# The first tile's second half of a scaled addition on GpSimd, at the end of three stages, the rest on VectorE

## The chip, the cores and the metric

The kernel runs on one core of one Trainium2 chip. The time is the device time of one execution in microseconds; lower is better. A core has a matrix engine (TensorE, PE in the profile), VectorE (DVE), ScalarE (ACT), GpSimd (POOL) and SyncE (SP), which here only issues DMAs. The engines run their own instruction streams and wait for each other on semaphores.

## The reference, cut to what matters

Two transformer-like blocks over 256 tokens of 1024 features. What matters here is the second block, all in float32:

```python
h = rms_norm(x, ffn1_pre_g)
x = x + 0.5 * rms_norm(swiglu(h, ffn1_w_gate, ffn1_w_up, ffn1_w_down), ffn1_post_g)
h = rms_norm(x, mix_pre_g)
...                                    # attention and a state-space mixer on h
x = x + rms_norm(mixed, mix_post_g)    # mixed = concat(attn, ssm) @ w_out
h = rms_norm(x, ffn2_pre_g)
x = x + 0.5 * rms_norm(swiglu(h, ffn2_w_gate, ffn2_w_up, ffn2_w_down), ffn2_post_g)
```

So three times a product y of a stage is normed and added to the rows: x = x + c * rs * (y * g), where g is a gain for each feature and rs the reciprocal root for each token.

## The kernel before, in words

The rows X lie in SBUF as two tiles of 128 tokens, X[:, tt, :], each 1024 wide; tt is the tile, hf the half of 512 features. The weights stream in by DMA from SyncE, ScalarE rounds each part to a high part (whi) and VectorE makes the rest (wlo); TensorE multiplies with both. The order on each engine is written out by hand, and semaphores link them.

At the end of a stage four products, one for each (tt, hf), stand in four PSUM banks (fa0 to fa3, wm0 to wm3, fb0 to fb3). `post_norm(i, names, loads)` (line 1827) on VectorE adds them to X. i is 4 behind the first feed-forward, 6 behind the mixing stage and 8 behind the second feed-forward. Its steps:

- `tile_mean` (1810, instruction 1814) prepares the first sum of squares of a tile; ScalarE makes the sums in `tile_stats` (1380) and the root in `tile_root` (1371).
- `gained(n)` (1836) multiplies bank n by the gain PG into the buffer XN2, 128x512.
- `tile_scale` (1820) takes the reciprocal of the root: the scale of each token, nst[:, i % 2, 8 + tt].
- `piece(n)` (1844) is one instruction on 128x512: X = XN2 * scale + X. It counts up the semaphore x_piece.

In VectorE's order: mean 0, gained 0, gained 1, scale 0, piece 0, piece 1, mean 1, gained 2, scale 1, piece 2, gained 3, piece 3. Behind stages 4 and 6 VectorE then waits for all pieces and counts up x_half and x_new, which release ScalarE's sums of squares for the next norm (1354).

Behind stages 4 and 6 TensorE turns X by `tile_transposes` (line 726; its instructions are 739, fillers 704): tile 0 half 0, tile 0 half 1, then tile 1 half 0 and half 1, each group of four transposes waiting for its piece by x_piece. Three filler matmuls stand before each group of tile 1. ScalarE copies the turned banks into XT's high part (`stream_hi`, 1412), and VectorE makes the low part (`stream_lo`, 1897), pair by pair; a pair can start only when tile 1's group has been turned too. Behind stage 4 VectorE first makes the small weights of the next product (`small_parts`, 1906 and 1907), TensorE waits for them, runs five fillers (704, ten records) and goes on.

Behind stage 8 X goes out in four stores of 256 KB: SyncE's two (line 627, half 0 of both tiles) wait for x_piece 9 and 11, ScalarE's two (line 1763, half 1) for x_piece 10 and 12.

GpSimd's last work in the kernel before is a set of masks near 877 us (lines 679 to 694); it is idle after that.

Of the kernel before, what the change touches and what calls it, by code (L numbers as in the profile page):

```python
# [8 lines left out]
T, D = 256, 1024  # L9
# [17 lines left out]
PIECES = {(0, 0): 2, (1, 0): 3, (1, 2): 3}  # L27
# [181 lines left out]
def before_in(ring, n):  # L209

    return next((m for m in range(n - 1, -1, -1) if ring[m] == ring[n]), None)
# [44 lines left out]
def reads_upto(i, who):  # L256

    return sum(1 for _, e in MAIN[:i + 1] if e == who)


def program(nc, x, panels1, experts, peer_u, peer_v, ffa, panels2, ffb, cols, conv_cols, w_low, w_gate_up, w_sgu, k12,
# [3 lines left out]
    ALU = mybir.AluOpType  # L265
# [5 lines left out]
    with ctx:  # L271
        def sb(name, shape, dt=f32):
            return ctx.enter_context(nc.sbuf_tensor(name, shape, dt))

        def sem(name):
            return ctx.enter_context(nc.semaphore(name))
# [9 lines left out]
        X = sb("X", [P, NT, D])  # L286
# [12 lines left out]
        nst = small[:, 0:20].rearrange("p (a n) -> p a n", a=2)  # L299
# [83 lines left out]
        XN2 = cut(NT, D)  # L383
# [55 lines left out]
        t_done = sem("t_done")  # L439
        t_read = [sem("t_read_0"), sem("t_read_1")]  # L440
        norm_sq, norm_ms, norm_sd, norm_out = sem("norm_sq"), sem("norm_ms"), sem("norm_sd"), sem("norm_out")
        x_new, x_half, x_piece = sem("x_new"), sem("x_half"), sem("x_piece")
        yf_ready, rs_ready, rs_spread = sem("yf_ready"), sem("rs_ready"), sem("rs_spread")
        gla_abs, gla_ln, gla_l, gla_e = sem("gla_abs"), sem("gla_ln"), sem("gla_l"), sem("gla_e")
        gla_kd, gla_state = sem("gla_kd"), sem("gla_state")
# [35 lines left out]
        def read_out(eng, name):  # L481

            i = MAIN_AT[name]
            who = MAIN[i][1]
            eng.wait_ge(main_read[who], reads_upto(i, who))
# [9 lines left out]
        def t_claim(pe, stage, j):  # L495

            i = before_in(T_BANK, T_AT[stage] + j)
            if i is not None:
                t_read_wait(pe, i)
# [75 lines left out]
        @block.sync  # L575
        def _(sp):
            for tt in range(NT):
                sp.dma_start(X[:, tt, :], x[0, P * tt:P * tt + P, :]).then_inc(x_in[tt], 16)
            sp.dma_start(C[:, 0:NCOLS], cols[:, 0:NCOLS]).then_inc(cols_in, 16)
            sp.dma_start(FINAL, cols[:, NCOLS:NCOLS + 8]).then_inc(cols_in, 16)  # L580
            sp.dma_start(WL, w_low).then_inc(low_in, 16)

            def wait_item_used(item):

                n = item - EXP0
                if n < 0:
                    sp.wait_ge(part_lo, 2 * item + 2)
                elif n < P // 2:
                    sp.wait_ge(h_done, 2 * n + 2)
                elif n < P:  # L590
                    sp.wait_ge(a_used, 2 * n + 2 - P)
                else:
                    sp.wait_ge(part_lo, 2 * (item - P) + 2)

            def load(item, src):
                before = before_in(ITEM_SLOT, item)
                if before is not None:
                    wait_item_used(before)
                sp.dma_start(raw[:, ITEM_SLOT[item], :], src).then_inc(slot_ready[ITEM_SLOT[item]], 16)

            for j in range(EXP0):
                load(j, panels1[j])

            def stream(item0, count, src, split0):

                for j in range(RING):
                    load(item0 + j, src[j])
                turns = (count - RING) // RING
                with sp.Fori(0, turns, 1) as i:
                    for s in range(RING):  # L610

                        sp.wait_ge(part_lo, i * (2 * RING) + (split0 + 2 * s + 2))
                        slot = ITEM_SLOT[item0 + s]
                        sp.dma_start(raw[:, slot, :], src[i * RING + (RING + s)]).then_inc(slot_ready[slot], 16)
                for j in range(RING * (turns + 1), count):
                    load(item0 + j, src[j])

            for j in range(P):
                load(EXP0 + j, experts[j])
            sp.dma_start(FG, row_post[0:1, :].broadcast_to([P, D])).then_inc(final_in, 16)  # L620
            stream(FFA0, FFI, ffa, S_FFA)
            for j in range(FFB0 - MIX0):
                load(MIX0 + j, panels2[j])
            stream(FFB0, FFI, ffb, S_FFB)
            for tt in range(NT):
                sp.wait_ge(x_piece, 8 + 2 * tt + 1)
                sp.dma_start(out[0, P * tt:P * tt + P, 0:512], X[:, tt, 0:512]).then_inc(out_done, 16)
            sp.wait_ge(out_done, 16 * 2 * NT)

# [2 lines left out]
        def _(pool):  # L632
# [36 lines left out]
            for n in range(2 * PICKS):  # L669
                if n >= BUFS:  # L670
# [23 lines left out]
            pool.affine_select(out=DB[:, P:384], in_=DB[:, P:384], compare_op=ALU.is_ge, fill=-1e32, base=P,  # L694
                               pattern=[[-1, T]], channel_multiplier=1).then_inc(pool_const2, 1)

        @block.tensor
        def _(pe):  # L700
            def keep_busy(out, n):

                for _ in range(n):
                    pe.matmul(out[:, 0:P], ident[:, :], ident[:, :], start=True, stop=True)
# [21 lines left out]
            def tile_transposes(stage, src, arrive, scales=None, order=range(NT), keep={}):  # L726

                pairs = dict(TSTAGES)[stage]
                for j in range(pairs):
                    t_claim(pe, stage, j)  # L730
                for tt in order:
                    for j in range(pairs):
                        keep_busy(t_bank(stage, pairs - 1 if (tt, j) == (1, 2) else 0)[:, P:2 * P], keep.get((tt, j), 0))
                        arrive(tt, j // 2)
                        for q in range(2):
                            c = slice(P * (2 * q + tt), P * (2 * q + tt) + P)
                            k = 2 * j + q
                            if scales is None:
                                last = pe.transpose(t_bank(stage, j)[:, c], src[:, tt, P * k:P * k + P], ident[:, :])
                            else:  # L740
                                last = pe.matmul(t_bank(stage, j)[:, c], src[:, tt, P * k:P * k + P], scales[:, tt, :],
                                                 start=True, stop=True)
                        if tt == order[-1]:
                            last.then_inc(t_done, 1)

            def tiles(src, n):

# [416 lines left out]
            feed_forward(S_FFA, 0, [f"fa{i}" for i in range(4)], between=lambda: (turn_back(2), turn_back(3)))  # L1164


            tile_transposes("mix", X, lambda tt, hf: pe.wait_ge(x_piece, 2 * tt + hf + 1), keep=PIECES)
            new_stream("mix")
            pe.wait_ge(small_split, 2)
            claim(pe, "dt")  # L1170
# [109 lines left out]
            for j in range(1, 4):  # L1280
# [10 lines left out]
            pe.wait_ge(part_lo, S_WM + 12)  # L1291
            last_two([bank(name) for name in names], (S_WM + 10, S_WM + 11), (stream_acts(NK - 2), stream_acts(NK - 1)),
                     part_used)
            tile_transposes("ffb", X, lambda tt, hf: pe.wait_ge(x_piece, 4 + 2 * tt + hf + 1), keep=PIECES)
            new_stream("ffb")
            feed_forward(S_FFB, NF, [f"fb{i}" for i in range(4)])

# [2 lines left out]
        def _(act):  # L1300
# [458 lines left out]
            warm_root(1)  # L1759
            tile_stats(8, *products_of("fb"))  # L1760
            for hf in range(2):
                act.wait_ge(x_piece, 8 + 2 * hf + 2)
                act.dma_start(out[0, P * hf:P * hf + P, 512:D], X[:, hf, 512:D]).then_inc(out_done, 16)


# [1 line left out]
        def _(dve):  # L1767
# [49 lines left out]
            def tile_scale(i, tt):  # L1817

                dve.wait_ge(norm_sd, NORM_ROOTS[i] + tt + 1)
                link(dve.reciprocal(nst[:, i % 2, 8 + tt:9 + tt], nst[:, i % 2, 6 + tt:7 + tt]))  # L1820
# [6 lines left out]
            def post_norm(i, names, loads):  # L1827

                dve.wait_ge(post_in, 16 * loads)

                def gained(n):

                    tt, hf = n // 2, n % 2
                    dve.wait_ge(main_done, MAIN_AT[names[n]] + 1)
                    dve.wait_ge(norm_sq, sum(NORM_PARTS[:i]) + n + 1)
                    read_done(dve.tensor_tensor(XN2[:, tt, 512 * hf:512 * hf + 512], bank(names[n]),
                                                PG[:, 512 * hf:512 * hf + 512], ALU.mult))

                def piece(n):

                    tt, hf = n // 2, n % 2
                    c = slice(512 * hf, 512 * hf + 512)
                    read_out(dve, names[n])
                    dve.scalar_tensor_tensor(X[:, tt, c], XN2[:, tt, c], nst[:, i % 2, 8 + tt:9 + tt], X[:, tt, c],
                                             ALU.mult, ALU.add).then_inc(x_piece, 1)

                tile_mean(i, 0, 1)
                gained(0)
                gained(1)
                tile_scale(i, 0)  # L1850
                piece(0)
                piece(1)
                tile_mean(i, 1, 3)
                gained(2)
                tile_scale(i, 1)
                piece(2)
                gained(3)
                piece(3)
                if i != 8:
                    dve.wait_ge(x_piece, 4 if i == 4 else 8)  # L1860
                    dve.sem_inc(x_half, 1)
                    dve.sem_inc(x_new, 1)

# [168 lines left out]
            for i in range(4):  # L2032
                hf, tt = i // 2, i % 2
# [656 lines left out]
```

## Time and profile before

| | us |
|---|---|
| median of 3 runs | 1432.86 (1432.69 to 1433.44) |
| the profiled execution | 1431.76 |
| its span, first to last instruction | 1430.0 |
| TensorE busy | 1398.2 (98%) |
| VectorE busy | 1021.1 (71%) |
| ScalarE busy | 521.8 (36%) |
| GpSimd busy | 274.9 (19%) |

All times of the trace are from the start of the span. A row of a timeline gives the start, the duration, the engine, the line, the operation, output and inputs by name with their shapes, how many instructions were merged, and in brackets the idle time ahead of it and who ended it. Two instructions of an engine can overlap in the records by about 0.1 us, since the next one starts while the last one drains. PE is the matmul record and PEld the weight load of the same instruction. The mean granted clock of TensorE was 0.999 of full speed, and everything ran on the one core.

### The profile page before, as it was taken

How to read it: one execution, taken by the hardware profiler on the slowest of the kernel's cores; microseconds unless marked ns; L12 is line 12 of the kernel's file. 1: busy time of each engine (PE TensorE's matmuls, PEld its weight loads, DVE VectorE, ACT ScalarE, POOL GpSimd, SP SyncE). 2: the span in 40 equal slices, each digit the busy share in tenths (PEclk: the TensorE clock that was granted, in tenths of full speed). 3: DMA queues.
4: the chain of work that ended last, by engine and by line, in shares of the span. 5: the costliest groups of instructions: out<-in, count | busy, mean ns of one | idle time of the engine just before them, and what ended most of it. 6: DMA issues, size and time to landing. Idle time of an engine off the chain costs nothing.

```text
span 1430.0 us, 23127 instructions
## 1 busy us (share of the span) xinstructions
PE 1398.2 (98%) x9058; PEld 1285.1 (90%) x9058; DVE 1021.1 (71%) x1836; ACT 521.8 (36%) x953; POOL 274.9 (19%) x235
## 2 busy tenths in 40 slices
PE   8999999999999999999999999999999999999998
PEld 7788889999999999999999998888889978888886
DVE  5566747989888886544444527788789897687887
ACT  5545464311433332000000006444457586544444
POOL 1000036344255454433333300000000000000000
PEclk9999999999999999999999999999999999999999
DMA  6445444699999999999999985555444333455552
GB/s 235 177 147 179 175 154 156 220 415 408 367 369 377 371 364 394 416 415 414 417 414 415 414 345 181 205 199 181 176 165 168 125 106 111 167 203 194 187 194 89
DMA packets 67211, 372.13 MB, mean 260 GB/s; under 512 B 7969, under 2 KB 8481, under 8 KB 34866
## 3 DMA queue, kind: packets, MB, share of 16 engines
q1 hardware_dynamic: 37440, 266.45, 49.0%
q0 software_dynamic: 27648, 100.68, 18.0%
q10 hardware_dynamic: 2034, 3.76, 0.7%
q8 instruction: 62, 1.02, 0.3%
q14 instruction: 27, 0.22, 0.0%
HBM read 369.81 MB, written 1.05 MB: 259 GB/s over the span
## 4 chain that ended last, share of the span: by engine, by line
PE 67%; DVE 14%; DMA 10%; ACT 6%; issue 3%; POOL 0%; DVEq 0%; SPq 0%; ACTq 0%; POOLq 0%
PE ps L754 26%; PE ps L1064 11%; PE ps L787 11%; PE ps L1013 10%; DMA raw<-in_experts 9%; PE ps L789 5%; ACT xt_plain L1527 3%; DVE wlo L569 2%; DVE hi_plain L2087 2%; DVE xt_plain L2201 2%; DVE lo_plain L2087 2%; DVE arena L2190 1%; DVE XT L1897 1%; PE ps L786 1%; DVE arena L2512 1%
## 5 line engine op out<-in xcount | busy, mean ns | idle before, releaser
L1064 PE MATMUL ps<-arena,raw 128*128 128x160 f32 x2048 | 282.1, 300 | 6.5 <-DMA raw<-in_experts 6.4
L1064 PEld LDWEIGHTS ps<-arena,raw 128*128 128x128 f32 x2048 | 278.6, 190 | 9.9 <-issue 6.0
L1013 PE MATMUL ps<-arena,raw 128*128 128x160 f32 x2048 | 284.8, 300 | 2.1 <-DVEq L2182 0.9
L1013 PEld LDWEIGHTS ps<-arena,raw 128*128 128x128 f32 x2048 | 279.2, 190 | 4.8 <-issue 2.1
L787 PE MATMUL ps<-XT,whi 128*128 128x512 f32 x704 | 249.5, 399 | 1.2 <-DVE wlo L569 1.0
L552 ACT ACTIVATE whi<-raw 128x1024 fp32r<-128x1024 f32 x152 | 159.7, 1060 | 237.5 <-PE ps L754 108.8
L569 DVE TENSOR_TENSOR wlo<-raw,whi 128x1024 fp32r<-128x1024 f32 x138 | 167.2, 1221 | 81.1 <-ACT whi L552 80.2
L754 PE MATMUL ps<-whi,XT 128*128 128x512 f32 x592 | 184.8, 393 | 3.3 <-DVE XT L1897 1.5
L789 PE MATMUL ps<-XT,wlo 128*128 128x256 f32 x616 | 172.8, 281 | 0.0
L1621 ACT ACTIVATE whi<-raw 128x1024 fp32r<-128x1024 f32 x96 | 101.9, 1062 | 155.7 <-PE ps L787 101.6
L787 PEld LDWEIGHTS ps<-XT,whi 128*128 128x128 f32 x704 | 129.4, 188 | 28.3 <-DVE wlo L569 2.1
L2364 DVE TENSOR_TENSOR wlo<-raw,whi 128x1024 fp32r<-128x1024 f32 x96 | 117.3, 1222 | 44.4 <-ACT whi L1621 44.4
L754 PEld LDWEIGHTS ps<-whi,XT 128*128 128x128 f32 x592 | 109.4, 188 | 30.6 <-issue 4.7
L754 PE MATMUL ps<-XT,whi 128*128 128x256 f32 x640 | 117.2, 285 | 2.7 <-DVE wlo L569 1.0
L789 PEld LDWEIGHTS ps<-XT,wlo 128*128 128x128 f32 x616 | 116.4, 189 | 3.2
L754 PE MATMUL ps<-wlo,XT 128*128 128x512 f32 x296 | 115.4, 390 | 0.0
L2108 DVE SCALAR_TENSOR_TENSOR arena<-hi_plain,arena 128x1024 f32<-128x1024 f32 x46 | 59.1, 1284 | 78.7 <-DMA hi_plain<-in_peer_v,arena 78.6
L2108 DVE SCALAR_TENSOR_TENSOR arena<-lo_plain,arena 128x1024 f32<-128x1024 f32 x47 | 60.4, 1285 | 63.7 <-DMA lo_plain<-in_peer_v,arena 63.0
L754 PEld LDWEIGHTS ps<-XT,whi 128*128 128x128 f32 x640 | 99.5, 192 | 3.7 <-issue 1.9
L754 PE MATMUL ps<-XT,wlo 128*128 128x256 f32 x320 | 90.5, 283 | 0.0
L672 POOL DMA_INDIRECT hi_plain<-in_peer_u,arena x48 | 69.0, 1438 | 105.8 <-DVE arena L2087 77.4
L672 POOL DMA_INDIRECT lo_plain<-in_peer_u,arena x48 | 62.1, 1293 | 59.4 <-DVE arena L2087 48.8
(312 smaller groups left out, 1861.4 us busy)
## 6 DMA issues: line engine op xcount, KB each, us to landing
raw<-in_experts SPq DMA_DIRECT2D x128, 1024.0 KB, 8.0
raw<-in_panels SPq DMA_DIRECT2D x58, 1024.0 KB, 4.9
raw<-in_ffa SPq DMA_DIRECT2D x33, 1024.0 KB, 4.9
raw<-in_ffb SPq DMA_DIRECT2D x33, 1024.0 KB, 4.8
arena<-in_row_post ACTq DMA_DIRECT2D x4, 512.0 KB, 4.9
X<-in_x SPq DMA_DIRECT2D x2, 512.0 KB, 5.3
hi_plain<-in_peer_u,arena POOLq DMA_INDIRECT x48, 9.0
lo_plain<-in_peer_u,arena POOLq DMA_INDIRECT x48, 9.9
```

The costliest lines, as they stand in the source:

```text
L552: act.activation(whi[:, buf(p), :], half(item_of(p), p % 2), ACT.Copy).then_inc(part_hi, 1)
L569: eng.tensor_tensor(low_weights(p), half(item_of(p), p % 2), whi[:, buf(p), :].bitcast(f32), ALU.subtract).then_inc(part_lo, 1)
L672: pool.indirect_dma_start(out=GATHERED[n % BUFS], out_offset=None, in_=(peer_u, peer_v)[n // PICKS][:, :], in_offset=bass.IndirectOffsetOn ...
L754: last = pe.matmul(out, x if w_moving else w, w if w_moving else x, start=start and n == 0, stop=stop and n == 2)
L787: last = pe.matmul(out, wh[:, k], XT[:, k], start=k == 0, stop=k == NK - 1)
L789: pe.matmul(out[:, T:], wl[:, k], XTh[:, k], start=False, stop=False)
L1013: last = pe.matmul(out[:, 0:TD], w[:, k], XF[:, k, :], start=k == 0, stop=k == NK - 1)
L1064: last = pe.matmul(t_bank("ffa", k // 2)[:, at:at + TD], w[:, P * k:P * k + P], G[:, c, :], start=False, stop=False, skip_group_check=True)
L1621: act.activation(whi[:, buf(q), :], half(item_of(q), q % 2), ACT.Copy)\
L2087: dve.tensor_tensor_reduce(u, u, XROWS[:, k // 32, :], 1.0, 0.0, ALU.mult, ALU.add, HS[:, k:k + 1])\
L2108: ins = dve.scalar_tensor_tensor(into, v, a, into, ALU.mult, ALU.add)
L2364: dve.tensor_tensor(wlo[:, buf(q), :], half(item_of(q), q % 2), whi[:, buf(q), :].bitcast(f32), ALU.subtract).then_inc(part_lo, 1)
```

## The change

In `post_norm` piece 1 (tile 0, half 1) leaves VectorE. GpSimd does it in two instructions, a scale of XN2 in place and an addition to X, with a wait on its own semaphore between them. It waits until VectorE has read all of bank 1 (`read_out`) and for the new semaphore first_scaled, which VectorE counts up behind scale 0 and ahead of piece 0; it counts up x_second. The counts of x_piece go from four to three for each stage, and whoever waited for the moved piece waits for x_second: TensorE's second group of tile 0, ScalarE's first store, and VectorE ahead of x_half and x_new. At stage 8 SyncE's two stores wait for counts 7 and 8 instead of 9 and 11.

```diff
             for tt in range(NT):
-                sp.wait_ge(x_piece, 8 + 2 * tt + 1)
+                sp.wait_ge(x_piece, 6 + tt + 1)
                 sp.dma_start(out[0, P * tt:P * tt + P, 0:512], X[:, tt, 0:512]).then_inc(out_done, 16)
...
+            for stage, i in enumerate((4, 6, 8)):
+                read_out(pool, ("fa1", "wm1", "fb1")[stage])
+                pool.wait_ge(first_scaled, stage + 1)
+                pool.tensor_scalar(XN2[:, 0, 512:D], XN2[:, 0, 512:D], nst[:, i % 2, 8:9], None, ALU.mult)\
+                    .then_inc(x_scaled, 1)
+                pool.wait_ge(x_scaled, stage + 1)
+                pool.tensor_tensor(X[:, 0, 512:D], X[:, 0, 512:D], XN2[:, 0, 512:D], ALU.add).then_inc(x_second, 1)
...
+            def piece_in(stage, tt, hf):
+
+                if (tt, hf) == (0, 1):
+                    pe.wait_ge(x_second, stage + 1)
+                else:
+                    pe.wait_ge(x_piece, 3 * stage + (1, 2, 3)[tt + hf])
...
-            tile_transposes("mix", X, lambda tt, hf: pe.wait_ge(x_piece, 2 * tt + hf + 1), keep=PIECES)
+            tile_transposes("mix", X, lambda tt, hf: piece_in(0, tt, hf), keep=PIECES)
...
-            tile_transposes("ffb", X, lambda tt, hf: pe.wait_ge(x_piece, 4 + 2 * tt + hf + 1), keep=PIECES)
+            tile_transposes("ffb", X, lambda tt, hf: piece_in(1, tt, hf), keep=PIECES)
...
             for hf in range(2):
-                act.wait_ge(x_piece, 8 + 2 * hf + 2)
+                act.wait_ge(*((x_piece, 9) if hf else (x_second, 3)))
                 act.dma_start(out[0, P * hf:P * hf + P, 512:D], X[:, hf, 512:D]).then_inc(out_done, 16)
...
                 tile_scale(i, 0)
+                dve.sem_inc(first_scaled, 1)
                 piece(0)
-                piece(1)
                 tile_mean(i, 1, 3)
...
                 if i != 8:
-                    dve.wait_ge(x_piece, 4 if i == 4 else 8)
+                    dve.wait_ge(x_piece, 3 if i == 4 else 6)
+                    dve.wait_ge(x_second, 1 if i == 4 else 2)
                     dve.sem_inc(x_half, 1)
                     dve.sem_inc(x_new, 1)
```

## Rows read from the trace of the kernel before

**Rows 1.** The page's busy times: us, share of the span, instructions.
```profile
PE 1398.2 (98%) x9058; PEld 1285.1 (90%) x9058; DVE 1021.1 (71%) x1836; ACT 521.8 (36%) x953; POOL 274.9 (19%) x235
```

**Rows 2.** Busy time by stretch: us, then each engine, TensorE's clock, DMA.
```profile
1056.00:1062.00 6.00, 5.38 (x38) 4.22 (x37) 5.59 (x13) 4.79 (x13) 0.00 (x0) 1.00 0.06 25
1233.00:1238.00 5.00, 4.64 (x35) 3.88 (x35) 4.59 (x11) 3.57 (x10) 0.00 (x0) 1.00 0.00 2
```

**Rows 3.** The chain that ended last, behind stage 4: start, us, what.
```profile
1060.82 0.02 DVEq L1862
...
1060.94 0.30 DVE HAh L1906
...
1061.27 0.43 DVE HAl L1907
...
1061.74 1.38 PE ps L704 x10
```

**Rows 4.** Timeline of VectorE behind stage 4.
```profile
1056.16 0.15 DVE L1820 RECIPROCAL small<-small 128x1 f32<-128x1 f32 x1
1056.35 1.42 DVE L1844 SCALAR_TENSOR_TENSOR X<-arena,small,X 128x512 f32<-128x512 f32 x2
1057.68 0.15 DVE L1814 TENSOR_SCALAR small<-small 128x1 f32<-128x1 f32 x1
...
1058.34 0.15 DVE L1820 RECIPROCAL small<-small 128x1 f32<-128x1 f32 x1
1058.53 0.75 DVE L1844 SCALAR_TENSOR_TENSOR X<-arena,small,X 128x512 f32<-128x512 f32 x1
...
1059.92 0.75 DVE L1844 SCALAR_TENSOR_TENSOR X<-arena,small,X 128x512 f32<-128x512 f32 x1
```

**Rows 5.** Timeline of TensorE's weight loads behind stage 4.
```profile
1057.82 0.42 PEld L739 LDWEIGHTS ps<-ident,X 128*128 128x128 f32 x4 [0.25 <-DVE X L1844]
1058.21 0.75 PEld L704 LDWEIGHTS ps<-ident 128*128 128x128 f32 x6
1059.34 0.42 PEld L739 LDWEIGHTS ps<-ident,X 128*128 128x128 f32 x4 [0.38 <-DVE X L1844]
...
1060.72 0.42 PEld L739 LDWEIGHTS ps<-ident,X 128*128 128x128 f32 x4 [0.25 <-DVE X L1844]
```

**Rows 6.** Timeline of ScalarE behind stage 4.
```profile
1057.24 0.19 ACT L1380 ACTIVATION_READ_ACCUMULATOR arena<-ps 128x1 f32 x1
1057.87 0.29 ACT L1371 ACTIVATE small<-small 128x1 f32<-128x1 f32 x1 [0.43 <-DVE small L1814]
```

**Rows 7.** GpSimd's groups: busy us, mean ns of one, idle before.
```profile
L694 POOL TENSOR_SCALAR_AFFINE_SELECT arena<-arena 128x256 f32<-128x256 f32 x1 | 0.4, 400 | 0.0
...
L692 POOL TENSOR_SCALAR_AFFINE_SELECT arena<-arena 128x128 f32<-128x128 f32 x1 | 0.3, 293 | 0.0
```

**Rows 8.** Lines by source (ns min/median/max), and both engines' timelines near 200 us.
```profile
L569 POOL TENSOR_TENSOR wlo<-raw,whi x14: 2377/2393/3377, 200.6 to 241.1; 128x1024 fp32r<-128x1024 f32 x14
...
200.64 5.72 POOL L569 TENSOR_TENSOR wlo<-raw,whi 128x1024 fp32r<-128x1024 f32 x2 [180.00 <-ACT whi L552]
...
200.88 3.22 DVE L2070 SCALAR_TENSOR_TENSOR arena<-X,small,arena 96x1024 f32<-96x1024 f32 x1 [2.49 <-DMA arena<-in_row_post]
...
L2108 DVE SCALAR_TENSOR_TENSOR arena<-hi_plain,arena x46: 1283/1284/1287, 575.0 to 835.2; 128x1024 f32<-128x1024 f32 x46
```

**Rows 9.** Timeline behind stage 6: ScalarE's root, its copies, VectorE's low parts.
```profile
1233.81 0.29 ACT L1371 ACTIVATE small<-small 128x1 f32<-128x1 f32 x1 [0.72 <-DVE small L1814]
...
1235.76 3.03 ACT L1412 ACTIVATE XT<-ps,C 128x256 fp32r<-128x256 f32 x8 [0.71 <-PE ps L739]
...
1236.96 3.22 DVE L1897 SCALAR_TENSOR_TENSOR XT<-ps,C,XT 128x256 fp32r<-128x256 f32 x8 [0.34 <-DVE X L1844]
```

**Rows 10.** The last addition, and landing time of ScalarE's stores (line 1763).
```profile
1426.79 0.75 DVE L1844 SCALAR_TENSOR_TENSOR X<-arena,small,X 128x512 f32<-128x512 f32 x1
...
DMA to landing us min/median/max: 2.0/2.0/2.0
```

More of the change, by code:

```diff
@@ L441, in program @@
         norm_sq, norm_ms, norm_sd, norm_out = sem("norm_sq"), sem("norm_ms"), sem("norm_sd"), sem("norm_out")
-        x_new, x_half, x_piece = sem("x_new"), sem("x_half"), sem("x_piece")
+        x_new, x_half, x_piece, x_second = sem("x_new"), sem("x_half"), sem("x_piece"), sem("x_second")
+        first_scaled, x_scaled = sem("first_scaled"), sem("x_scaled")
         yf_ready, rs_ready, rs_spread = sem("yf_ready"), sem("rs_ready"), sem("rs_spread")
```

## The prediction

> **What bounds the kernel now.** Start at the busy shares: TensorE is busy for 98% of the span and GpSimd for 19% [rows 1]. So time can be won or lost only where TensorE waits. The change touches three such places, the ends of stages, where the normed product is added to the rows X: after the first feed-forward (A, 1054 to 1062 us), after the mixing stage (B, 1230 to 1240 us) and after the second feed-forward (C, 1421 to the end). The stretches by time show TensorE 5.4 of 6 us busy in A and 4.6 of 5 us in B, at a granted clock of 1.00, with GpSimd idle [rows 2]; part of TensorE's work there is filler. The chain of waits says who leads in A: VectorE, link after link, up to the low part of the small weights at 1061.27; TensorE's fillers start 0.04 us after that ends [rows 3]. The VectorE timeline shows what it does in A: scale of tile 0, two additions of 0.75 us back to back (1.42 together, so the next may start 0.67 after the first), the mean and product of tile 1, its scale, two more additions [rows 4]. The TensorE loads show its side: four transposes take 0.39, three fillers 0.75, and the waits for X are only 0.25 and 0.38 [rows 5]. So two transpose groups of tile 1 can't start closer than 1.14 us apart.
>
> **What the change removes, adds and moves, in A.** *Removed:* the second addition of tile 0, 0.67 us of VectorE. Not all of it comes back. Scale 1 needs ScalarE's root, which waited 0.43 us for VectorE's mean; its fourth sum was there at 1057.43 [rows 6]. With 0.10 for its own wait (estimate: 0.04 from the mean's end to the root in rows 4 and 6, taken higher) the root starts at 1057.53 instead of 1057.87. Gain on VectorE: 0.34, and piece 2 becomes due at 1058.19 instead of 1058.53.
>
> *Added on VectorE:* one semaphore step ahead of piece 0. The step at 1060.82 held the next instruction to 1060.94 [rows 3]: 0.12. Behind it stand piece 0 and all that follows, but as the root is set by ScalarE, the 0.12 only moves piece 0 to 1056.47 and is hidden by the root's wait (without that cover, 0.12 each time). At stages A and B the extra wait on GpSimd ahead of the two steps that release the norm of the next stage costs nothing as long as GpSimd ends before piece 3.
>
> *Added on GpSimd:* a scale and an addition of 128x512, one after the other. No such scale stands in the trace. Its nearest rows are the one-input selects: 400 ns for 256 elements and 293 for 128 [rows 7], 0.84 ns an element, so 0.61 for 512; with the scale read from memory I take 0.7 (bounds 0.6 and 1.2, the addition's). The addition: 2393 ns for 1024 elements [rows 8], so between 1.2 (half) and 1.34 (with 0.29 of it fixed, which is about what the 128-element select takes in all); I take 1.3. Between the two 0.1 for the semaphore.
>
> *Do they run beside VectorE?* This decides the case, and one place in the trace answers it. At 200.88 VectorE starts a three-operand addition of 96x1024, two inputs in SBUF, while GpSimd is in a subtraction since 200.64. It takes 3.22 us; the same form elsewhere takes 1284 ns [rows 8]. So its work ran from 202.82, 0.2 before GpSimd's 2.38 us (the group's least) was over at 203.02; and GpSimd's next subtraction took 3377 instead of 2393. One blocked the other, both ways. Pieces 0, 2 and 3 are of that form; the products with a PSUM input, the means and the reciprocals are not, and I take them as free.
>
> The Trainium skill, SBUF — State Buffer, "Who interferes with whom", says it as a rule against this change: a VectorE instruction with two SBUF inputs and a GpSimd instruction that reads SBUF exclude each other, and whichever starts first keeps the port to its end. The trace agrees, with 3.22 against 1.28 us. By that rule the sum is the forecast below; were it not so, the rival "no block" would be.
>
> **The sum.** In A, VectorE first: piece 0 holds GpSimd's scale back to 1057.2; scale to 1057.9; addition 1058.0 to 1059.3, and VectorE may go on at 1059.1. Piece 2, due at 1058.19, waits 0.9 and ends at 1059.85 instead of 1059.28. Gained 0.34, lost 0.91: pieces 2, 3 and the small weights come 0.57 later. TensorE: tile 0's second group starts at 1059.35, tile 1's groups 1.14 and 2.28 later, at 1060.49 and 1061.63 instead of 1059.34 and 1060.72. The last is 0.91 late, but TensorE stood idle after it until 1061.74 [rows 3, 5], so the stage is late by the small weights: **+0.57**.
>
> B is the same with times 175.95 later. There the root waited longer, 0.72 [rows 9], so its new start is set by the mean and piece 2 is due at 1233.95, just when GpSimd's addition starts (1233.95): close to a tie. If GpSimd's comes first, tile 1's first group starts at 1236.44 instead of 1235.28 (1.16 late), ScalarE's first two copies of the stream, 1235.76 before, end near 1237.67, and VectorE's first low part, 1236.96 before [rows 9], starts near 1237.70: **+0.75**. No slack follows, since from there the chain runs on VectorE into TensorE.
>
> C: the end is piece 3 at 1426.79 and the store behind it, 2.0 us [rows 10]. The store of tile 0's second half moves to about 1426.2, still ahead of piece 3 (1427.4) on ScalarE's queue, and nothing is queued behind it but the last store. SyncE's two stores count one piece less and move with piece 2. So the end moves with piece 3: **+0.57**.
>
> Sum 0.57 + 0.75 + 0.57 = 1.9 us. The profiled execution took 1431.76 (span 1430.0 and 1.76 around it), so it would be 1433.7; the median of the three runs was 1432.86, 1.1 more, so I forecast 1434.8. What a measurement of this kernel can tell from no change is about 0.2%, 2.87 us: up to 1435.73 counts as the same.
>
> **The rivals.**
> - *GpSimd first (0.24).* Its scale and piece 0 are released within a few hundredths of each other, and no row says who wins. If the scale does, it runs 1056.45 to 1057.15, piece 0 ends at 1057.7, GpSimd's addition runs 1057.65 to 1058.95, the mean comes at 1057.62, nearly as before, piece 2 is due at 1058.47, waits to 1058.75 and pieces 2 and 3 end 0.2 to 0.3 late. In B tile 1's first group is 0.9 late and the stream 0.45. Together 0.3 + 0.45 + 0.3 = +1.1: 1434.0.
> - *Slower by over 0.2%: piece 2 slips in between scale and addition (0.20).* This happens where GpSimd's scale takes over about 0.9 us in A (over 0.7 in B), or starts late. Then the addition starts only after piece 2, at 1058.94, and ends at 1060.3. VectorE loses little (piece 3 waits to 1060.1), but TensorE's three groups start at 1060.35, 1061.49 and 1062.63; the fillers follow at 1063.03 instead of 1061.74, +1.3. In B the same +1.5 through the stream (first group 1237.24, low part 1238.5). In C +0.2 to 0.4, since the last two stores then go out nearly together. Sum +3.1: 1436.0. For it: the scale's price is an extrapolation. Against it: the one-input rows are short. Where it happens in B alone the sum is 0.57 + 1.5 + 0.57 = 2.6, 1435.5.
> - *No block (0.10).* If GpSimd's addition takes in only what it needs and VectorE isn't held, pieces 2 and 3 come 0.34 early: A -0.3, C -0.3. GpSimd ends at 1058.6 (0.7 + 0.1 + 1.3 after 1056.5), tile 1's groups come 0.45 and 0.3 late, which is within TensorE's idle time in A and about nothing in B. Sum -0.6: 1432.3. Against it: the 3.22 us in rows 8.
> - *A granted clock that falls (0.03).* TensorE will wait 1.6 us in one piece for tile 0's second half. Rows 2 show 1.00 through the present, shorter gaps. If half the clock doubled the 2.28 us of transposes and fillers behind it (an estimate; no row shows such a stretch), half of that beyond TensorE's slack, about 1 us would be added in each of A and B: 1436.8.
>
> **How the numbers follow.** Forecast 0.43 (the sum of B's two forms lies in 1434.8 to 1435.5), GpSimd first 0.24, piece 2 in between 0.20, no block 0.10, clock 0.03. The range of 8 in 10 leaves out most of the no-block case and the far end of the slow ones: 1432.6 to 1436.4. Slower by over 0.2%: most of the case in between (0.14), the clock (0.03) and a little of the forecast's upper form (0.04), 0.21. Faster by over 0.2% would need 2.87 us, while all that can be gained is 0.34 to 0.56 at each of three places: 0.03 for what I don't see. Same: 0.76.
>
> **What would show it.** In the profile after: GpSimd's scale (0.7, or 1.3 with the wait in it) and addition (1.3) three times; piece 0 at 750 ns (forecast) or near 1250 (GpSimd first); piece 2 near 1650 ns instead of 750, and 750 with a long piece 3 in the slow case; root 1 starting 0.34 earlier; TensorE waiting 1.6 us for GpSimd's addition at the second transpose group of tile 0; the last store 0.57 later after the last matmul. Pieces at 750 throughout would make the prediction wrong on its main point; a scale over 0.9 us would make it too low.

## The result, and the profile after

The median went from 1432.78 to 1440.2 us (four executions each): the ratio is 1.0048, with a 95% interval of 1.0036 to 1.006. The change makes the kernel slower by 7.4 us; 1.9 were forecast. The profiled execution took 1440.13, its span 1438.4.

The page's busy times, and GpSimd's two new groups (busy us, mean ns of one, idle before), answer [rows 1] and [rows 7]:

```profile
PE 1398.9 (97%) x9058; PEld 1286.9 (89%) x9058; DVE 1020.5 (71%) x1833; ACT 522.1 (36%) x953; POOL 280.6 (20%) x241
...
L701 POOL TENSOR_SCALAR arena<-arena,small 128x512 f32<-128x512 f32 x3 | 6.3, 2112 | 542.0 <-DVEq L1866 542.0
L704 POOL TENSOR_TENSOR X<-X,arena 128x512 f32<-128x512 f32 x3 | 3.8, 1266 | 0.3
```

VectorE has three instructions less, as meant. But the scale takes 2.11 us on GpSimd, and no busy time has grown enough for 8.4 us of span.

**Where the time went.** Executions of this kernel differ by some us ahead of stage 4 already, in parts that the change leaves alone, so spans can't be compared here to a few tenths. What can be compared is the time from one stage's end to the next. As a mark I take ScalarE's first sum of squares in each of the three places. The timeline of ScalarE, before and then after:

```profile
1054.03 0.60 ACT L1380 ACTIVATE arena<-ps 128x512 f32<-128x512 f32 x1
...
1420.93 0.60 ACT L1380 ACTIVATE arena<-ps 128x512 f32<-128x512 f32 x1 [2.80 <-PE ps L754]
```

```profile
1055.01 0.60 ACT L1395 ACTIVATE arena<-ps 128x512 f32<-128x512 f32 x1
...
1231.61 0.60 ACT L1395 ACTIVATE arena<-ps 128x512 f32<-128x512 f32 x1 [1.63 <-PE ps L769]
...
1425.26 0.60 ACT L1395 ACTIVATE arena<-ps 128x512 f32<-128x512 f32 x1 [2.80 <-PE ps L769]
```

(The mark of B before is at 1229.68.) The differences, for every kernel of this study:

| kernel, profiled execution | A to B | B to C | C to the end |
|---|---|---|---|
| before | 175.65 | 191.25 | 9.07 |
| the change | 176.60 | 193.65 | 13.14 |
| e1, stages 4 and 6 only | 176.62 | 193.75 | 9.05 |
| e2, stage 8 only | 175.69 | 191.19 | 13.18 |
| e3, a memset at the end | 175.60 | 191.18 | 13.98 |
| e4, the change with fillers | 176.55 | 192.46 | 13.09 |
| e5, GpSimd instructions tried beside | 175.66 | 191.22 | 9.08 |
| e6, a memset at stage 6 | 175.62 | 191.21 | 9.03 |
| e7, scale released by piece 0 | 178.52 | 192.84 | 13.44 |
| e8, before without VectorE's steps | 175.30 | 190.60 | 9.06 |
| e9, GpSimd's addition alone, 4 and 6 | 175.65 | 191.45 | 9.07 |
| e10, e1 with fillers | 176.64 | 192.46 | 9.09 |
| e11, e3 without the gathers | 175.67 | 191.22 | 9.06 |
| e12, e9 without VectorE's steps | 174.91 | 191.29 | 9.03 |

Where nothing was changed the columns repeat within 0.09 us, over executions whose first mark lies anywhere from 1043.0 (e11) to 1061.0 (e5). e5, e6, e7, e9, e11 and e12 ran once each, with the profiler: 1438.72, 1433.28, 1441.32, 1432.74, 1420.64 and 1433.17 us. What they say is read from the columns; e5's 7 us and e11's 11 us lie ahead of A. The change costs 0.95 us behind stage 4 (A), 2.40 behind stage 6 (B) and 4.07 at the end (C), 7.4 together, which is the difference of the medians.

**In A**, the timelines of GpSimd, VectorE and TensorE's loads, answering [rows 4] and [rows 5]:

```profile
1057.54 2.11 POOL L701 TENSOR_SCALAR arena<-arena,small 128x512 f32<-128x512 f32 x1 [178.68 <-DVEq L1866]
1059.73 1.26 POOL L704 TENSOR_TENSOR X<-X,arena 128x512 f32<-128x512 f32 x1
...
1057.45 0.75 DVE L1859 SCALAR_TENSOR_TENSOR X<-arena,small,X 128x512 f32<-128x512 f32 x1 [0.16 <-DVE small L1835]
...
1059.03 0.75 DVE L1859 SCALAR_TENSOR_TENSOR X<-arena,small,X 128x512 f32<-128x512 f32 x1
...
1060.42 1.12 DVE L1859 SCALAR_TENSOR_TENSOR X<-arena,small,X 128x512 f32<-128x512 f32 x1
1062.20 0.30 DVE L1922 CAST HAh<-arena 128x256 fp32r<-128x256 f32 x1 [0.65 <-DVE X L1859]
...
1058.26 0.42 PEld L747 LDWEIGHTS ps<-ident,X 128*128 128x128 f32 x4 [0.32 <-DVE X L1859]
1061.05 0.42 PEld L747 LDWEIGHTS ps<-ident,X 128*128 128x128 f32 x4 [2.37 <-POOL X L704]
...
1063.21 0.47 PEld L747 LDWEIGHTS ps<-ident,X 128*128 128x128 f32 x4
```

VectorE's piece 0 starts 0.09 us ahead of GpSimd's scale. Piece 2 (1059.03) runs in 0.75 us beside the scale; piece 3 meets GpSimd's addition and takes 1.12. TensorE waits 2.37 us for the addition, and the groups of tile 1 follow it with no wait: the last of all groups starts 8.20 us behind the mark, 6.69 before.

VectorE's own chain did get shorter. The first product and ScalarE's root of tile 1 before, then the same and VectorE's second scale after:

```profile
1057.75 0.68 DVE L1836 TENSOR_TENSOR arena<-ps,arena 128x512 f32<-128x512 f32 x1
```

```profile
1058.19 0.68 DVE L1851 TENSOR_TENSOR arena<-ps,arena 128x512 f32<-128x512 f32 x1
1058.84 0.16 DVE L1835 RECIPROCAL small<-small 128x1 f32<-128x1 f32 x1
...
1058.51 0.29 ACT L1386 ACTIVATE small<-small 128x1 f32<-128x1 f32 x1
```

Before, the root was there at 1058.16 and the scale of tile 1 started at 1058.34, when VectorE came out of the product: the product held it, not the root. After, the root ends at 1058.80 and the scale follows 0.04 later. Behind the mark the root comes 0.34 earlier (3.50 against 3.84), and piece 2 comes 0.48 earlier (4.02 against 4.50).

**In B** the same gap of 2.36 us stands ahead of the second group, and the groups behind it are slow. TensorE's loads, and busy time by stretch (the last three columns are the granted clock, DMA share, GB/s), answering [rows 2]:

```profile
1237.61 0.64 PEld L747 LDWEIGHTS ps<-ident,X 128*128 128x128 f32 x4 [2.36 <-POOL X L704]
...
1239.52 0.87 PEld L747 LDWEIGHTS ps<-ident,X 128*128 128x128 f32 x4
```

```profile
1234.00:1236.00 2.00, 1.40 (x10) 0.93 (x8) 1.94 (x5) 1.91 (x6) 1.90 (x1) 1.00 0.02 4
1236.00:1238.00 2.00, 0.38 (x2) 0.39 (x3) 1.96 (x3) 0.35 (x1) 1.48 (x2) 0.94 0.02 4
1238.00:1240.00 2.00, 2.00 (x12) 2.00 (x11) 0.11 (x1) 0.00 (x0) 0.00 (x0) 0.50 0.00 0
1240.00:1242.00 2.00, 2.00 (x15) 2.00 (x14) 0.65 (x2) 1.60 (x5) 0.00 (x0) 0.71 0.00 0
```

Behind the gap the granted clock is 0.50, which is the level of 1.2 GHz, and four transposes take 0.87 us where the like group took 0.47 in A at 1.00 (1063.21).

VectorE's start in B also differs from before for a reason that the change doesn't contain. In the kernel before, 0.23 us pass between the first two products of B in which VectorE waits for nothing that the profile shows:

```profile
1231.50 0.69 DVE L1836 TENSOR_TENSOR arena<-ps,arena 128x512 f32<-128x512 f32 x1 [0.23 <-issue]
```

This idle time stands there in every execution in which VectorE's instructions up to B are those of before (before, e2, e3, e5, e6, e11), and in none of the others. Without it the scale of tile 0 comes 0.32 earlier behind the mark (2.11 in the change, 2.43 before). Why it goes is open; in B each kernel of the second kind has these 0.3 us of VectorE's chain to the good.

**At the end** the last piece is over at 1431.76, 6.50 us behind the mark, 0.11 earlier than before; ScalarE's stores land 2.1 us after they are issued. All that would end the program near 1434. It ends at 1438.4. The instructions that end the program stand under line 271, the `with ctx:` around the whole of it. GpSimd's drain, at the end of its stream, is one of them. Duration in ns, start in us, after:

```profile
L271 POOLq DRAIN  x1: 8258/8258/8258, 1429.9 to 1429.9; - x1
...
L271 SPq DRAIN  x1: 7/7/7, 1434.1 to 1434.1; - x1
...
L271 SPq EVENT_SEMAPHORE  x1: 17/17/17, 1438.3 to 1438.3; - x1
```

SyncE is done at 1434.1 and passes the common end at 1438.3. In between only GpSimd's drain is under way: it ends at 1438.16, 6.95 us behind GpSimd's last addition (1429.94 and 1.27). The same drain stands in the trace of the kernel before, behind the last mask (877.43 and 0.40), where nothing waited for it:

```profile
L271 POOLq DRAIN  x1: 7922/7922/7922, 876.9 to 876.9; - x1
```

### The profile page after: what moved, and what is told of

It reads as the page before. It is cut to its first block, busy times and chain, and to the rows that moved or that the text cites. A ratio compares the mean times of both kernels' runs of the same rounds, so it can differ in the third digit from the quotient of the medians.

```text
span 1438.4 us, 23133 instructions
## 1 busy us (share of the span) xinstructions
PE 1398.9 (97%) x9058; PEld 1286.9 (89%) x9058; DVE 1020.5 (71%) x1833; ACT 522.1 (36%) x953; POOL 280.6 (20%) x241
## 3 DMA queue, kind: packets, MB, share of 16 engines
HBM read 369.81 MB, written 1.05 MB: 258 GB/s over the span
## 4 chain that ended last, share of the span: by engine, by line
PE 65%; DVE 14%; DMA 11%; ACT 6%; issue 2%; POOL 1%; DVEq 0%; SPq 0%; ACTq 0%; POOLq 0%
PE ps L769 26%; DMA raw<-in_experts 11%; PE ps L802 11%; PE ps L1079 10%; PE ps L1028 10%; PE ps L804 5%; ACT xt_plain L1542 3%; DVE wlo L570 2%; DVE hi_plain L2103 2%; DVE xt_plain L2217 2%; DVE lo_plain L2103 2%; DVE arena L2206 1%; DVE XT L1913 1%; PE ps L801 1%; DVE arena L2528 1%
## 5 line engine op out<-in xcount | busy, mean ns | idle before, releaser
L701 POOL TENSOR_SCALAR arena<-arena,small 128x512 f32<-128x512 f32 x3 | 6.3, 2112 | 542.0 <-DVEq L1866 542.0
```

## The experiments

### The end: e1, e2, e3, e6, e11

e1 takes the change at stage 4 and 6 alone, e2 at stage 8 alone. The edit of e1 (e2 is its mirror; the counts of x_piece follow):

```diff
-            for stage, i in enumerate((4, 6, 8)):
+            for stage, i in enumerate((4, 6)):
...
-                dve.sem_inc(first_scaled, 1)
+                if i in (4, 6):
+                    dve.sem_inc(first_scaled, 1)
                 piece(0)
+                if i not in (4, 6):
+                    piece(1)
```

> The change at stages 4 and 6 alone; behind stage 8 VectorE does all four pieces again. Theory (the end's loss is GpSimd's drain, which lasts 6.95 us behind its last instruction and was hidden 540 us before the end): the last addition ends where it did and the span ends 2.4 us behind it, as before the change. Of the 7.4 us, 4.1 are gone: 1436.0, +3.3 against before (0.93 at stage 4, 2.4 at stage 6), less where TensorE's clock does not fall behind stage 6. Rival (the loss at the end is no drain but two stores that collide on ScalarE's queue): the same time here, so this run says only how much belongs to the end; the late memset tells the two apart. Rival (the whole is one loss before stage 8, by what GpSimd does to the weight stream): near 1440.

Measured: 1435.83 us, ratio 1.002 (1.001 to 1.003). The end is 9.05 as before, A and B are those of the change.

> The change at stage 8 alone. Theory (drain): GpSimd's addition ends some 0.1 us before the last piece and the program ends 6.95 us behind it instead of 2.4: +4.0 us, 1436.8, with the granted clock at 1.00 up to the last matmul. The two parts, this and the change at stages 4 and 6 alone, add up to the whole change (7.4). Rival (stores collide): the stores land over 4 us later than the last piece and the drain is short.

Measured: 1435.98 us, ratio 1.0025 (1.0014 to 1.0035), with 13.18 to the end and nothing in A and B. The columns add up: 0.97 + 2.50 + 4.11 is 7.6, for 7.4 of the whole. The medians, each against its own runs of before (1432.66), add up to 6.5 only (3.2 and 3.3), which their intervals allow. GpSimd's drain in e2 is as long as in the change, 8.26 us from the addition's start.

e3 tells drain from stores. One instruction is added to the kernel before, at the end of GpSimd's stream:

```diff
+            pool.wait_ge(x_piece, 12)
+            pool.memset(LS[:, 6:7], 0.0)
```

> The kernel before with one added instruction: a GpSimd memset of one unused column behind the last of the twelve additions. No work moves, nobody waits for it. Theory (GpSimd's drain at the program's end lasts 6.95 us from its last instruction): the memset ends near 1427.7 of the span, so the span ends near 1427.7 + 6.95 + 0.2 = 1434.9 instead of 1430.0: +4.9, 1437.7. Rival (the drain's length comes from the two big instructions, or the end is late because of the stores): the memset is over in 0.1 us and costs nothing, 1432.8.

Measured: 1437.67 us, ratio 1.0033 (1.0024 to 1.0043): +5.0, as the theory says, for a memset of 0.10 us that nobody waits for. Its drain, from line 271's instructions:

```profile
L271 POOLq DRAIN  x1: 7050/7050/7050, 1430.7 to 1430.7; - x1
```

e6 is the same memset behind the eighth addition (wait for x_piece 8), in the middle of the program.

> The kernel before with one added GpSimd memset of one unused column behind the eighth addition, at the end of stage 6, some 190 us before the end. Theory (a drain of 7 us behind GpSimd's last instruction, dear only where nothing else is left to do): the drain stands at 1237 to 1244 of the span and the last stage ends in 9.07 us from its first sum, as before. Rival (any late use of GpSimd lengthens the end by 4 to 5 us): 13 to 14.

Measured: 9.03 us from the mark of C to the end. The drain is as long, but stands under 190 us of other work:

```profile
L271 POOLq DRAIN  x1: 7050/7050/7050, 1238.2 to 1238.2; - x1
```

So the length of the drain is the same, and the place of GpSimd's last instruction decides what it costs. e11 asks what makes it long. It is e3 with the gathers gone:

```diff
-                pool.indirect_dma_start(
-                    out=GATHERED[n % BUFS], out_offset=None, in_=(peer_u, peer_v)[n // PICKS][:, :],
-                    in_offset=bass.IndirectOffsetOnAxis(ap=ROWS[:, n % PICKS:n % PICKS + 1], axis=0))\
-                    .then_inc(row_here[n % BUFS], 16)
+                pool.memset(GATHERED[n % BUFS], 0.5).then_inc(row_here[n % BUFS], 16)
```

> The run with the late memset again, with GpSimd's 192 gathers replaced by memsets of the same buffers, so the expert rows and the output are wrong. Theory (the drain is long because GpSimd has issued indirect DMAs; at the head of the program, ahead of any, it took 0.19 us): the drain behind the late memset takes well under 1 us and the last stage ends in 9.1 us from its first sum instead of 13.98. Rival (7 us is what a drain of GpSimd costs late in any program): 7.05 us and 13.98 as before. The stretch of the gathers itself gets shorter; that says nothing here.

Measured: the drain takes 0.17 us, and the end comes 9.1 us behind the mark (1409.84, span 1418.9).

```profile
L271 POOLq DRAIN  x1: 171/171/171, 1416.5 to 1416.5; - x1
```

The 7 us need the gathers, though the last of them is issued at 828 us (line 672 in the kernel before), 600 us earlier. Whether any DMA issued by GpSimd does it or only the indirect kind was not tried.

### The clock: e4 and e10

```diff
-PIECES = {(0, 0): 2, (1, 0): 3, (1, 2): 3}
+PIECES = {(0, 0): 2, (0, 2): 9, (1, 0): 3, (1, 2): 3}
```

> The whole change with nine more filler matmuls (some 2.3 us) on TensorE ahead of the second pair group of tile 0, behind stages 4 and 6, where TensorE idled 2.37 us for GpSimd. Theory (the wait itself costs 0.9 us behind stage 4 and about 1.1 behind stage 6, and the fall of the granted clock to 0.50 for 3.4 us behind stage 6 costs the other 1.3): the clock stays at 1.00, stage 6 costs about 1.1 instead of 2.4, and the time is 1438.8, 1.3 below the change; runs scatter less. Rival (the clock's fall is not what TensorE's chain waits for, or comes whatever fills the gap): 1440.1 as with the change.

Measured: 1439.21 us, ratio 1.0037 (1.0024 to 1.0049). The stretches behind stage 6, where the change had 0.50 and 0.71:

```profile
1240.00:1242.00 2.00, 1.88 (x18) 1.69 (x17) 0.85 (x1) 0.06 (x1) 0.30 (x1) 1.00 0.00 0
1242.00:1244.00 2.00, 1.99 (x19) 1.82 (x18) 1.11 (x3) 2.00 (x6) 0.00 (x0) 1.00 0.00 0
```

B to C is 192.46: B costs 1.21 and not 2.40. The clock's share there is 1.2 us. The medians (1440.2 and 1439.21) go the same way, but their intervals overlap; the column decides. e10 has the same fillers with the change at stages 4 and 6 alone.

> The change at stages 4 and 6 alone, with nine fillers on TensorE in the gap behind each. No drain at the end, no fall of the clock. Theory: from first sum to first sum 176.6 and 192.45, 9.05 to the end, +2.15 against before: 1434.8, and 1.2 us or a part of it below the same without fillers (1435.8). Rival (the fall of the clock doesn't come from the gap): a stretch at 0.50 still shows behind stage 4 or 6, and the time is that of the run without fillers.

Measured: 1435.77 us, ratio 1.0016 (1.0006 to 1.0026); the columns are those expected, 176.64, 192.46 and 9.09. The time is 1.0 above the forecast, with its own runs of before at 1433.31, 0.65 above those of e1. That the fillers are worth 1.2 in the median can't be told from these runs (e1 had 1435.83 without them). The gap does not always bring the fall: in the change and e1 it came in B and not in A, in e7 in A (A to B 178.52) and not in B, each with a gap of 2.4 to 2.7 us; with fillers in neither, in e4 and e10. e7's stretches in A, busy time and granted clock:

```profile
1061.00:1063.00 2.00, 1.84 (x10) 1.84 (x11) 1.31 (x3) 0.00 (x0) 0.10 (x1) 0.59 0.02 4
1063.00:1065.00 2.00, 2.00 (x12) 2.00 (x12) 0.25 (x2) 1.14 (x4) 0.00 (x0) 0.56 0.00 0
```

### GpSimd's prices: e5 and e7

e5 adds 29 instructions on free memory while GpSimd is idle anyway, four rounds of seven forms:

```diff
+            one(pool.memset(XS[:, 0, :], 1.0))
+            for _ in range(4):
+                one(pool.tensor_scalar(A, A, eps, None, ALU.mult))
+                one(pool.tensor_scalar(A, A, 1.5, None, ALU.mult))
+                one(pool.tensor_scalar(A[:, 0:256], A[:, 0:256], eps, None, ALU.mult))
+                one(pool.tensor_scalar(A[:, 0:256], A[:, 0:256], 1.5, None, ALU.mult))
+                one(pool.tensor_tensor(A, A, B2, ALU.add))
+                one(pool.tensor_tensor(A, A, eps.broadcast_to([P, 512]), ALU.mult))
+                one(pool.tensor_tensor(A[:, 0:256], A[:, 0:256], B2[:, 0:256], ALU.add))
```

> The kernel before with 29 added GpSimd instructions on free memory during the first feed-forward, one after the other: four times a scale of 128x512 with the factor read from memory, the same with a constant factor, both on 128x256, an addition of 128x512, a product of 128x512 with one column broadcast, an addition of 128x256. Theory (the scale is dear by its form, the factor from memory, and 2.11 us behind the stages is its own price): 2.1 us here too, about half with the constant, and the price hangs on the 512 elements (256 take about 1.2). Rival (its own price is about 0.7 and the rest was waiting for VectorE's additions, first piece 0 and then piece 2): the shortest of four is about 0.7 with either factor. The addition should take 1.27 where VectorE leaves it alone.

By source line, ns of the shortest, middle and longest of four: the scale with its factor from memory, with a constant, the latter on 256, and the addition:

```profile
L710 POOL TENSOR_SCALAR arena<-arena,C x4: 1616/1898/2853, 886.0 to 921.3; 128x512 f32<-128x512 f32 x4
L711 POOL TENSOR_SCALAR arena<-arena x4: 1491/1714/2127, 888.1 to 923.0; 128x512 f32<-128x512 f32 x4
...
L713 POOL TENSOR_SCALAR arena<-arena x4: 854/933/1914, 892.8 to 926.8; 128x256 f32<-128x256 f32 x4
L714 POOL TENSOR_TENSOR arena<-arena x4: 1278/1558/1697, 893.9 to 927.7; 128x512 f32<-128x512 f32 x4
```

Neither theory held as put. The scale's own price is 1.5 to 1.6 us, with either factor: not 2.1, and not 0.7. An element costs it 2.5 ns ((1491 - 854) / 256), three times the 0.84 of the selects in [rows 7]. The addition has the price forecast.

e7 says what the other 0.55 of the 2.11 is:

```diff
-                pool.wait_ge(first_scaled, stage + 1)
+                pool.wait_ge(x_piece, 3 * stage + 1)
```

> The whole change, but GpSimd's scale is released by piece 0's end instead of by the semaphore step ahead of it, so that it starts about 0.65 us later and never beside piece 0. Theory (the scale takes 2.11 by its form): it still takes 2.11, all behind it comes 0.65 later, and the stages cost 1.6 and 3.0 instead of 0.95 and 2.4. Rival (0.6 of the 2.11 was the wait for piece 0): it takes 1.5, ends where it did, and the stages cost 0.95 and 2.4 as with the change.

```profile
L701 POOL TENSOR_SCALAR arena<-arena,small x3: 1562/1564/1576, 1058.2 to 1429.5; 128x512 f32<-128x512 f32 x3
```

The rival held for the scale: 1.56 us. So 0.55 was the wait for piece 0, all three times. The stages' costs came as neither side put them. The release by piece 0 comes a little late, GpSimd's addition ends 0.3 later than in the change, and B, where the clock stayed at 1.00 here, costs 1.59: 0.3 more than e4's 1.21, and a little. A, where the clock fell, costs 2.87: without the change's 0.95 and the 0.3 of the later release, the fall is worth about 1.6 there (an estimate from these three).

### What a faster GpSimd would have given: e9 and e12

e9 is e1 without GpSimd's scale (three lines less), e12 takes VectorE's wait and steps behind piece 3 away as well, as e8 does.

> GpSimd at stages 4 and 6 only, and its scale left out: it adds the unscaled half to the rows, so the second half of tile 0 is wrong. GpSimd's part is then one addition, 0.1 + 1.26 us, with 0.55 of waiting for piece 0 ahead of it. Theory (the stages are late only because GpSimd's two instructions end 2.9 us later than VectorE's piece did, and VectorE's own chain did get shorter): the addition ends 3.9 us behind the stage's first sum instead of 5.98, TensorE's groups are 0.2 us late or less, the pieces 2 and 3 come 0.25 to 0.3 early, and stage 4 takes 175.4 from first sum to first sum against 175.65 before, stage 6 191.2 against 191.25. Rival (having GpSimd read beside VectorE costs VectorE more than the piece saved): stage 4 takes 176 or more.

The timelines of GpSimd and VectorE in A, then in B:

```profile
1057.33 1.84 POOL L701 TENSOR_TENSOR X<-X,arena 128x512 f32<-128x512 f32 x1 [178.74 <-DVEq L1865]
...
1057.28 0.75 DVE L1857 SCALAR_TENSOR_TENSOR X<-arena,small,X 128x512 f32<-128x512 f32 x1 [0.16 <-DVE small L1833]
...
1232.94 1.27 POOL L701 TENSOR_TENSOR X<-X,arena 128x512 f32<-128x512 f32 x1 [173.77 <-DVEq L1865]
...
1232.89 1.86 DVE L1857 SCALAR_TENSOR_TENSOR X<-arena,small,X 128x512 f32<-128x512 f32 x1 [0.16 <-DVE small L1833]
```

The two exclude each other, and here both orders are seen: in A VectorE goes through in 0.75 and GpSimd takes 1.84 instead of 1.27; in B GpSimd goes through in 1.27 and piece 0 takes 1.86, though its record starts 0.05 earlier. In A the addition ends 4.34 us behind the mark and not at the expected 3.9, since VectorE was first and the wait came on top. The stages cost 0.00 and 0.20, against the expected -0.25 and -0.05; B has the 0.3 us of the missing idle time in its favour. In A the gain is there at piece 3, which ends 0.37 earlier behind the mark than before, but the small weights do not start earlier. The chain of waits of e9 in A:

```profile
1061.14 0.05 DVEq L1879
1061.19 0.45 issue
```

VectorE's step behind piece 3, which now waits for GpSimd's semaphore too, holds the next for 0.50 us (1061.14 to 1061.64), 0.11 before. GpSimd's addition was over at 1059.17, so the semaphore had its count by then; what fills the 0.45 us the profile doesn't show. e12 takes the step out.

> GpSimd's addition alone at stages 4 and 6 (its scale left out, so the second half of tile 0 is wrong), and VectorE without its wait and its two steps behind piece 3; ScalarE waits for the pieces and for GpSimd itself. Theory (VectorE's chain gained 0.37 us by the moved piece at stage 4 and lost 0.39 to the wait on GpSimd's semaphore there, which held it 0.50 us instead of 0.11): 0.65 us of idle are gone and stage 4 takes 174.95 from first sum to first sum, 0.35 below the kernel before without steps (175.30) and 0.7 below the kernel before. Rival (something else holds TensorE there): 175.3 or more. At stage 6 the order of GpSimd's addition and piece 0 decides: 190.3 if VectorE is first, 190.9 if GpSimd is.

Measured in A: 174.91, as expected, 0.74 below before. Taking the steps away gives 0.74 here and 0.35 in the kernel before (e8), so the other 0.39 is what the moved piece had gained and the longer step had eaten. That settles A, in one execution of each. In B: 191.29 against the 190.9 expected for GpSimd first. Piece 0 waited 0.51 us for its scale and then took 1.50; why its release came later there is open.

### A version that beats both, by little: e8

```diff
-                if i != 8:
-                    dve.wait_ge(x_piece, 4 if i == 4 else 8)
-                    dve.sem_inc(x_half, 1)
-                    dve.sem_inc(x_new, 1)
...
-            norm_stats(5, tiles, [lambda: act.wait_ge(x_half, 2), lambda: act.wait_ge(x_new, 4)])
+            norm_stats(5, tiles, [lambda: act.wait_ge(x_piece, 4), lambda: None])
```

(and norm_stats(7, ...) waits for x_piece 8).

> The kernel before with VectorE's own wait and the two semaphore steps behind piece 3 taken away; ScalarE waits for the pieces themselves. They stood on the chain at both stages, between the last piece and the small weights or the first low part. Theory (at these two places TensorE follows VectorE's chain, so what VectorE is spared there comes back in full): 0.27 us less at stage 4 and 0.25 at stage 6, first sums 175.4 and 191.0 apart, -0.5 us, 0.04%, under what the rounds can tell. Rival (TensorE's transposes or ScalarE's copies hold the stages as well): 175.65 and 191.25 as before.

Measured: 1431.35 us, ratio 0.999 (0.9981 to 0.9998), against 1433.31 for the kernel before: the interval ends just below 1. The columns give -0.35 and -0.65, 1.0 us together, twice what was expected, and C as before; the other 1.0 between the medians is not explained by them. B gives more than its 0.25 because the 0.23 us of idle time between its first two products are gone too:

```profile
1231.43 1.29 DVE L1836 TENSOR_TENSOR arena<-ps,arena 128x512 f32<-128x512 f32 x2
```

The scale of tile 0 starts 2.10 us behind the mark and not 2.43, which is 0.33, and the steps are 0.25 more: 0.58 of the 0.65. VectorE's links at these two places do come back nearly in full.

## Why the prediction was wrong, point by point

- **C, the step that failed most.** "So the end moves with piece 3: +0.57", against 4.07. Piece 3 ended 0.11 earlier. The sum looked at who waits for GpSimd's output, and not at what GpSimd itself does when its stream ends. e3 shows the mechanism alone (+4.9 in the column), e6 that it is free elsewhere, e11 that the gathers make it long. It could be read beforehand: in the trace of before the drain takes 7.92 us from 876.9, 7.0 of them behind the last mask. It was nowhere among the rivals.
- **GpSimd's price, a term mis-sized.** The scale was put at 0.7, at most 1.2, from selects of 128 and 256 elements. It costs 1.56, and 2.11 with the wait for piece 0. The addition was right (1.3; 1.26). The two end 5.98 us behind the mark of A, where piece 1 ended 3.74 behind it. "a scale over 0.9 us would make it too low" was the right alarm.
- **A and B.** With the late scale the rival "piece 2 slips in between" came true in its shape: piece 2 undisturbed, piece 3 long (1.12 against 0.75), TensorE's groups late one after another. It gave +1.3 and +1.5; A was 0.95 and B 1.21 without the clock. But piece 2 slipped in beside the scale and not between the two, so the addition could start 0.19 earlier than the rival put it (4.72 us behind the mark of A against 4.91) and its group 0.28 earlier (6.04 against 6.32); and the groups of tile 1 followed each other by 1.05 and 1.11 us, not 1.14. That accounts for A; in B the 0.3 us of the missing idle time helped as well.
- **The clock.** A rival at 0.03, with the right mechanism: a gap of 2.4 us, half clock behind it. Its price, 1 us, was near the 1.2 measured in B. The gap was put at 1.6 us; being 2.4 it deserved more than 0.03. It came in one of the two places in three of the profiled executions with an unfilled gap, those of the change, e1 and e7.
- **Who goes first.** VectorE in the change, by 0.09 us, as forecast. e9 shows that it is a tie that can fall the other way.
- **The blocking.** Right where VectorE's addition meets GpSimd's addition: piece 3 took 0.37 more here, piece 0 1.11 more in e9. The rule of the Trainium skill, SBUF — State Buffer, "Who interferes with whom", agrees with these. But piece 2 ran in 0.75 us from 1059.03 in the middle of GpSimd's scale (1057.54 to 1059.65), and the scale was not lengthened by it: e7's scale, beside piece 2 in the same way, took 1.56, no more than the shortest in e5. By the exclusive lock of that section of the Trainium skill, one of them should have waited. Why neither did is open. On VectorE's side the blocking wasn't what cost: its chain was off the path once TensorE waited for GpSimd. On GpSimd's side 0.55 us of waiting for piece 0 lay on that path, and the sum had counted it.
- **The extra wait on GpSimd.** It "costs nothing as long as GpSimd ends before piece 3" was wrong at stage 4: GpSimd had ended, and the step held VectorE 0.50 us where it had held it 0.11 (e9, and e12 against e8). In the change itself it lay beside TensorE's wait. At stage 6 it didn't appear.
- **The gain.** The root came 0.34 earlier as worked out, but piece 2 came 0.48 earlier: before, VectorE's own product held the scale of tile 1 and not the root. The term was a little too small. e9 and e12 show that 0.37 of it reaches the end of piece 3, if GpSimd needs only 1.3 us.

## What to carry to other kernels

Before a late piece of work goes to an idle engine, look at what the engine does when its program ends: here a 0.1 us memset cost 5 us because GpSimd had gathered rows, the last of them 600 us earlier, and its drain of 7 us was no longer hidden. Price an instruction by a row of its own form on that engine, or measure it beside the kernel first; here the scale took 1.56 us and not 0.7, and A lost 0.95, where e9, without the scale, lost nothing. And when a change opens a gap on TensorE, count the clock behind it too, or fill the gap.

## What the runs showed of the hardware that was not expected

- GpSimd's drain at the end of its stream lasts 6.95 to 7.05 us behind its last instruction where it has issued 192 indirect DMAs (the kernel before, the change, e3, e6), and 0.17 us where it has not (e11).
- A one-input scale of 128x512 in float32 takes GpSimd 1.49 to 1.62 us, more than an addition of two inputs (1.28). The Trainium skill, GPSIMD Engine Reference, "Engine selection", calls one-input operations roughly line-rate; here 256 more elements cost 637 ns (e5), 2.5 ns an element, three times the 0.84 of the selects, and the measurement decides.
- After TensorE had stood idle for 2.4 to 2.7 us the granted clock went to 0.50 for 3.4 us in one of two places (the change, e1, e7), at 1.2 us of the program's time in B; nine filler matmuls in the gap kept it at 1.00 (e4, e10).
